# Up projection by seven products: the rounded and the low moving part of two products in one matmul of 512 columns

## The chip, the core and the metric

The kernel runs on one core of a Trainium2 chip. Its time is the device time of the whole kernel in microseconds, the median of the runs shown.

## What is computed

An encoder block on 512 tokens of width 2048: two groups of attention heads with one input and one output projection, then an MLP with squared ReLU. The change touches only the first matmul of the MLP:

```python
h = rms_norm(x, g_pre_mlp[l]) * (1.0 + sc_m) + sh_m       # (512, 2048)
y = jnp.square(jax.nn.relu(h @ w_mlp_in[l])) @ w_mlp_out[l]   # w_mlp_in (2048, 8192)
x = x + gt_m * rms_norm(y, g_post_mlp[l])
```

All of it is float32.

## The kernel before

**Float32 by three products.** Each float32 operand is held as a rounded part (type fp32r, names with `hi`) and what is left of it (`lo`). A product is the sum of three matmuls: rounded by rounded, rounded weight by low activations, low weight by rounded activations. ScalarE (ACT) makes the rounded part of a weight (`su_hi`, line 1303), VectorE (DVE) the low part (`su_low`, line 2053), in a ring of four slots `hi[s]`, `lo[s]` of 1024 columns.

**Seven products.** The up projection is done by blocks of 256 output features. After the first four, which are done plainly, there are 28 blocks (`SU_BLOCKS`). In each, the weight (2048 x 256) is seen as 2 x 2 quarters of 1024 x 128, and the transposed activations as 2 x 2 quarters of 1024 x 256, and the block is put together from seven products of a weight combination by an activation combination (Strassen's scheme in Winograd's form) in place of eight. A product is numbered `e`, 0 to 6. Its moving part is `B[e]` (line 2799), a rounded and a low half, each 8 slices (`KH`) of 256 columns (`HALF_T`). Products 3 and 6 take theirs from `h2_hi` and `h2_lo` directly (quarters 1,0 and 0,1; the second of these was overwritten with a combination).

**Where the sums go.** PSUM has banks of 512 float32 columns. A block uses half of three of them: X is bank 6 or 7 in turn, Y bank 4, Z bank 5. Products 0, 2, 4 and 6 add up in X, 1 and 5 in Y, 3 stands alone in Z. On the way ACT copies X after product 0, Y after product 1 and X after product 2 into `c_a` and `c_b` in SBUF (`snap` 0, 1, 2), and DVE adds Z after product 3, X after product 4 and Y after product 5 to them (`corner` 0, 1, 2). Product 6 leaves the last quarter in X, which ACT reads itself (`square_rest`).

**The order on each engine** is the order of the program, and semaphores tie them. In block i:
- PE: products 0 to 6. Product 2 waits for snap 0, product 4 for snap 2, product 6 for corner 1, product 1 for corner 2 of the block before, each product for the low part of its weight (`su_lo`).
- ACT: weight 3 rounded, `square_rest` of block i-1, snap 0, weight 4, snap 1, weight 5, snap 2, weight 6, y_out of block i-1 rounded (`pair_hi`), weights 0, 1 and 2 of block i+1, `square_tops` of block i. The rounding of a weight waits until the product four before has released the slot.
- DVE: low part 3, `sum_four`, low part 4, the four mixes of y of block i-1 (`mix_pair`), low part 5, a piece of the gate (`gate_part`), low part 6, low part of y_out of i-1 (`pair_lo`), corner 0, `sum_one` for block i+1, low part 0, corner 1, low part 1, `sum_two`, `sum_three`, corner 2, low part 2.
- SyncE issues the four loads of 512 KB of a block as the steps above free their buffers (line 649), GpSimd stores y_out.

`sum_one` to `sum_four` (line 2056) make the weight combinations, in SBUF. In the last group (`LAST`, the last four blocks) `mix_pair` does nothing, and y_out is done in two operations of 512 columns. The stage that follows is the down projection (`dn_products`, lines 2848 to 2850), whose matmuls all have 512 columns.

Of the kernel before, what the change touches and what calls it, by code (L numbers as in the profile page):

```python
# [27 lines left out]
T = 512  # L28
NT = T // P
D = 2048  # L30
KD = D // P
# [65 lines left out]
KH = KD // 2  # L97
# [59 lines left out]
def build(nc, a, out, x1_dram, y_dram):  # L157
    with ExitStack() as ctx:
# [14 lines left out]
        def small(name, shape):  # L173
# [50 lines left out]
        o_hi, o_lo = sb("o_hi", 52, [KD, T], F32R), sb("o_lo", 84, [KD, T], F32R)  # L224
        h2_hi, h2_lo = sb("h2_hi", 52, [KD, T], F32R), sb("h2_lo", 84, [KD, T], F32R)

# [48 lines left out]
                                 for n, ats in (("one", (152, 160)), ("two", (168, 196)), ("three", (142, 188))))  # L275
        four_f = quarter(sb("h2_lo_f", 84, [KD, T]), 0, 1)
        c_a, c_b = sb("c_a", 150, [2, HALF_T]), sb("c_b", 204, [2, HALF_T])
        rows_m = sb("rows_m", 204, [COLS])
# [197 lines left out]
        X = lambda i: bank[6 + i % 2][:, 0:HALF_T]  # L476
        Y, Z = bank[4][:, 0:HALF_T], bank[5][:, 0:HALF_T]

        def at_dn(g, np, u):
# [338 lines left out]
        def _(act):  # L818
# [486 lines left out]
            def snap(g, i, n):  # L1305

                dst, src = ((c_a[:, 0, :], X(i)), (c_b[:, 1, :], Y), (c_a[:, 1, :], X(i)))[n]
                act.wait_ge(w_used, at_su(g, i, n).count(1, 1))
                if n == 0 and not (isinstance(g, int) and su_count(g, i, 1) == 0):
                    act.wait_ge(y_done, pair_n(g, i, 2))  # L1310
                nc.scalar.activation(dst, src, ACT.Copy).then_inc(su_snap, 1)

            def square_tops(g, i):

                act.wait_ge(su_c, su_count(g, i, 3, 3))
                flat_a = c_a[:].rearrange("p a n -> p (a n)")
                nc.scalar.activation(flat_a, flat_a, ACT.Relu).then_inc(relu_done, 1)
                nc.scalar.activation(c_b[:, 1, :], c_b[:, 1, :], ACT.Relu, scale=-1.0).then_inc(relu_done, 1)
                act.wait_ge(relu_done, su_count(g, i, 2, 1 + 2 * SU_FIRST))
                act.wait_ge(y_ready, pair_n(g, i))  # L1320
                nc.scalar.activation(y_mix[:, 0:2, :].rearrange("p a n -> p (a n)"), flat_a, ACT.Square).then_inc(y_done, 1)

            def square_rest(g, i):

                act.wait_ge(w_used, at_su(g, i, 6).count(1, 1))
                nc.scalar.activation(c_b[:, 0, :], X(i), ACT.Relu, scale=-1.0).then_inc(su_x, 1)
                act.wait_ge(su_x, su_count(g, i, 1, 1))
                act.wait_ge(relu_done, su_count(g, i, 2, 2 + 2 * SU_FIRST))
                nc.scalar.activation(y_mix[:, 6:8, :].rearrange("p a n -> p (a n)"), c_b[:].rearrange("p a n -> p (a n)"), ACT.Square).then_inc(y_done, 1)
# [114 lines left out]
        def _(dve):  # L1444
# [633 lines left out]
            def corner(g, i, n):  # L2078

                dst, src, e = ((c_a[:, 0, :], Z, 3), (c_b[:, 1, :], X(i), 4), (c_a[:, 1, :], Y, 5))[n]  # L2080
                dve.wait_ge(w_used, at_su(g, i, e).count(1, 1))
                dve.wait_ge(su_snap, su_count(g, i, 3, n + 1))
                tt(dst, src, dst, ALU.add).then_inc(su_c, 1)  # L2083

# [8 lines left out]
            def su_block(g, i):  # L2093
# [3 lines left out]
                su_low(g, i, 3)  # L2097
                sum_four(g, i)
                su_low(g, i, 4)
                mix_pair(g, i - 1)  # L2100
# [51 lines left out]
            def finish(u):  # L2152

                if u == 0:
                    corner(LAST, PAIRS - 1, 2)
                if u == 5:
                    gate_part(LAST, PAIRS - 1)
# [177 lines left out]
        def _(pe):  # L2335
# [456 lines left out]
            def up_block(f, before=lambda j: None, rest=range(UNITS_D)):  # L2792
                for j in rest:
# [3 lines left out]
                    unit_columns(w, up_set(f), h2_hi, h2_lo, QROWS * j, j == 0, j == UNITS_D - 1)  # L2797

            B = (h2_at(0, 0), t_one, t_two, h2_at(1, 0), t_three, h2_at(1, 1), t_four)

            def su_block(g, i):

                first = isinstance(g, int) and su_count(g, i, 1) == 0
                into = (X(i), Y, X(i), Z, X(i), Y, X(i))
                for e in range(SLOTS):
                    w = at_su(g, i, e)
# [5 lines left out]
                    if e == 1:  # L2812
                        wait_su(pe, su_c, g, i, 3)
                    if e in (2, 4):
                        pe.wait_ge(su_snap, su_count(g, i, 3, e - 1))
                    if e == 6:
                        pe.wait_ge(su_c, su_count(g, i, 3, 2))
                    if first and e in (1, 6):
                        pe.wait_ge(t_ready, 3 if e == 1 else 4)
                    pe.wait_ge(su_lo, su_count(g, i, SLOTS, e + 1))  # L2820
                    s, opens = w.slot(), e in (0, 1, 3)
                    for k in range(KH):
                        cols = slice(k % 4 * P, (k % 4 + 1) * P)
                        wh, wl = hi[s][:, k // 4, cols], lo[s][:, k // 4, cols]
                        bh, bl = (x[:, k, :] for x in B[e])
                        mm(into[e], wh, bh, start=opens and k == 0, stop=False, skip_group_check=not opens)  # L2826
                        mm(into[e], wh, bl, start=False, stop=False, skip_group_check=not opens)  # L2827
                        ins = mm(into[e], wl, bh, start=False, stop=k == KH - 1, skip_group_check=not opens)  # L2828
# [43 lines left out]
            def free_banks(i):  # L2872
# [3 lines left out]
                if i == 2:  # L2876
                    pe.wait_ge(su_c, 3 * SU_BLOCKS)

# [260 lines left out]
```

## Time and profile before

| | |
|---|---|
| median of 3 runs | 2010.45 us (2009.76 to 2010.79) |
| profiled execution | 2010.1 us, span 2008.1 us |
| PE busy | 1980.6 us, 99% of the span |
| PE weight load busy | 1734.6 us, 86% |
| DVE busy | 1720.9 us, 86% |
| ACT busy | 1006.4 us, 50% |
| DMA | 433.31 MB, mean 216 GB/s |
| up projection by seven products | about 809 to 1376 us |
| down projection | about 1376 to 1992 us |

PE is TensorE's matmuls, DVE VectorE, ACT ScalarE, POOL GpSimd, SP SyncE. In the profile, a matmul's record is longer than the distance to the next one (0.28 us against 0.12), as matmuls are pipelined and their ends modelled: the cost of one is the distance between starts. The same holds in a smaller way for DVE and ACT, where records of chained operations overlap by 0.08 to 0.1 us. Idle time of an engine stands in square brackets behind the row of the operation that ended it, with what released it.

### The profile page before, as it was taken

How to read it: one execution, taken by the hardware profiler on the slowest of the kernel's cores; microseconds unless marked ns; L12 is line 12 of the kernel's file. 1: busy time of each engine (PE TensorE's matmuls, PEld its weight loads, DVE VectorE, ACT ScalarE, POOL GpSimd, SP SyncE). 2: the span in 40 equal slices, each digit the busy share in tenths (PEclk: the TensorE clock that was granted, in tenths of full speed). 3: DMA queues.
4: the chain of work that ended last, by engine and by line, in shares of the span. 5: the costliest groups of instructions: out<-in, count | busy, mean ns of one | idle time of the engine just before them, and what ended most of it. 6: DMA issues, size and time to landing. Idle time of an engine off the chain costs nothing.

```text
span 2008.1 us, 30631 instructions
## 1 busy us (share of the span) xinstructions
PE 1980.6 (99%) x11143; PEld 1734.6 (86%) x11143; DVE 1720.9 (86%) x2051; ACT 1006.4 (50%) x1425; POOL 159.8 (8%) x174
## 2 busy tenths in 40 slices
PE   7999999999999999999999999999999999999998
PEld 6887888878888878999999999998888888888886
DVE  7897988788877788999999999988998898898866
ACT  6464223698732474565656565655343334333322
POOL 0000000267400000000000000000300000000000
PEclk9999999999999999999999999999999999999999
DMA  9988778500487745667666767669746546556552
GB/s 378 351 299 304 249 218 254 180 1 22 150 268 255 239 157 189 216 213 232 211 233 210 234 208 233 210 207 349 242 173 251 205 171 251 191 185 251 179 177 84
DMA packets 260467, 433.31 MB, mean 216 GB/s; under 512 B 27680, under 2 KB 155296, under 8 KB 247456
## 3 DMA queue, kind: packets, MB, share of 16 engines
q1 hardware_dynamic: 242576, 361.42, 53.0%
q0 software_dynamic: 15936, 63.97, 8.7%
q10 hardware_dynamic: 1872, 6.82, 0.9%
q8 instruction: 52, 0.85, 0.2%
q14 instruction: 31, 0.25, 0.0%
HBM read 367.68 MB, written 64.49 MB: 215 GB/s over the span
## 4 chain that ended last, share of the span: by engine, by line
PE 90%; DVE 4%; ACT 3%; issue 1%; DMA 1%; SPq 0%; POOL 0%; ACTq 0%; POOLq 0%; DVEq 0%
PE bank L2826 9%; PE bank L2828 9%; PE bank L2827 9%; PE bank L2848 9%; PE bank L2850 9%; PE bank L2849 9%; PE bank L2349 6%; PE bank L2351 6%; PE bank L2350 6%; PE bank L2909 1%; PE bank L2908 1%; PE bank L2907 1%; PE bank L2364 1%; PE bank L2363 1%; PE bank L2362 1%
## 5 line engine op out<-in xcount | busy, mean ns | idle before, releaser
L1384 ACT ACTIVATE hi<-w 128x1024 fp32r<-128x1024 f32 x168 | 178.4, 1062 | 264.9 <-PE bank L2850 194.4
L2848 PE MATMUL bank<-hi,y_use 128*128 128x512 f32 x784 | 306.6, 391 | 0.0
L2849 PE MATMUL bank<-lo,y_use 128*128 128x512 f32 x784 | 305.1, 389 | 0.0
L2850 PE MATMUL bank<-hi,y_use 128*128 128x512 f32 x784 | 305.1, 389 | 0.0
L1303 ACT ACTIVATE hi<-a 128x1024 fp32r<-128x1024 f32 x196 | 206.6, 1054 | 154.5 <-DVE a L2056 142.0
L2053 DVE TENSOR_TENSOR lo<-a,hi 128x1024 fp32r<-128x1024 f32 x196 | 239.1, 1220 | 43.6 <-ACT hi L1303 43.2
L2826 PE MATMUL bank<-h_hi,hi 128*128 128x256 f32 x896 | 253.7, 283 | 1.0 <-DVE c_b L2083 1.0
L2828 PE MATMUL bank<-h_hi,lo 128*128 128x256 f32 x896 | 253.6, 283 | 0.0
L2827 PE MATMUL bank<-h_lo,hi 128*128 128x256 f32 x896 | 253.6, 283 | 0.0
L825 ACT ACTIVATE hi<-raw 128x1024 fp32r<-128x1024 f32 (+2 forms) x119 | 119.6, 1009 | 229.6 <-PE bank L2351 80.2
L2168 DVE TENSOR_TENSOR lo<-w,hi 128x1024 fp32r<-128x1024 f32 x168 | 205.2, 1228 | 31.3 <-ACT hi L1384 30.1
L1452 DVE TENSOR_TENSOR lo<-raw,hi 128x1024 fp32r<-128x1024 f32 (+2 forms) x118 | 135.6, 1151 | 62.4 <-ACT hi L825 61.2
L2849 PEld LDWEIGHTS bank<-lo,y_use 128*128 128x128 f32 x784 | 147.2, 188 | 31.4 <-issue 1.0
L2848 PEld LDWEIGHTS bank<-hi,y_use 128*128 128x128 f32 x784 | 147.2, 188 | 31.3 <-issue 1.0
L2850 PEld LDWEIGHTS bank<-hi,y_use 128*128 128x128 f32 x784 | 147.1, 188 | 30.7
L2826 PEld LDWEIGHTS bank<-h_hi,hi 128*128 128x128 f32 x896 | 172.0, 192 | 1.2 <-DVE c_b L2083 1.2
L2827 PEld LDWEIGHTS bank<-h_lo,hi 128*128 128x128 f32 x896 | 172.0, 192 | 0.0
L2828 PEld LDWEIGHTS bank<-h_hi,lo 128*128 128x128 f32 x896 | 172.0, 192 | 0.0
L2056 DVE TENSOR_TENSOR a<-a,a 128x1024 f32<-128x1024 f32 x112 | 134.5, 1221 | 2.0
L2248 DVE TENSOR_TENSOR acc<-bank,acc 128x1024 f32<-128x1024 f32 x84 | 102.3, 1217 | 0.0
L2349 PE MATMUL bank<-hi,h_hi 128*128 128x512 f32 x256 | 100.6, 393 | 0.7 <-DVE lo L1452 0.7
L2351 PE MATMUL bank<-hi,h_lo 128*128 128x512 f32 x256 | 99.7, 389 | 0.0
(406 smaller groups left out, 4690.3 us busy)
## 6 DMA issues: line engine op xcount, KB each, us to landing
w<-in_w_mlp_out SPq DMA_DIRECT2D x128, 512.0 KB, 4.9
a<-in_w_mlp_in SPq DMA_DIRECT2D x112, 512.0 KB, 4.5
y_use<-y_dram SPq DMA_DIRECT2D x53, 1024.0 KB, 9.1
y_dram<-y_out POOLq DMA_DIRECT2D x28, 1792.0 KB, 6.8
w_turned<-in_w_ada_t SPq DMA_DIRECT2D x32, 1024.0 KB, 6.9
raw<-in_w_mod SPq DMA_DIRECT2D x64, 512.0 KB, 4.8
raw<-in_w_ada SPq DMA_DIRECT2D x36, 512.0 KB, 4.7
raw<-in_w_out SPq DMA_DIRECT2D x32, 512.0 KB, 4.6
```

The source lines that it names most:

```text
L1303: nc.scalar.activation(hi[w.slot()][:], su_weight(i, e)[:].rearrange("p (q k) n -> p q (k n)", q=QROWS), ACT.Copy).then_inc(hi_ready, 1)
L1384: nc.scalar.activation(hi[w.slot()][:], weight(np, i, h)[:], ACT.Copy).then_inc(hi_ready, 1)
L2053: tt(lo[w.slot()][:], src, hi[w.slot()][:].bitcast(F32), ALU.subtract).then_inc(su_lo, 1)
L2168: tt(lo[w.slot()][:], weight(np, i, h)[:], hi[w.slot()][:].bitcast(F32), ALU.subtract).then_inc(dn_lo, 1)
L2349: mm(acc[t][:], xh, hi[s][:, q, :], start=first and q == 0, stop=False)
L2351: ins = mm(acc[t][:], xl, hi[s][:, q, :], start=False, stop=last and q == QROWS - 1)
L2826: mm(into[e], wh, bh, start=opens and k == 0, stop=False, skip_group_check=not opens)
L2827: mm(into[e], wh, bl, start=False, stop=False, skip_group_check=not opens)
L2828: ins = mm(into[e], wl, bh, start=False, stop=k == KH - 1, skip_group_check=not opens)
L2848: mm(bank[b + m][:], yh, hi[s][:, q, :], start=j == 0, stop=False)
L2849: mm(bank[b + m][:], yh, lo[s][:, q, :], start=False, stop=False)
L2850: ins = mm(bank[b + m][:], yl, hi[s][:, q, :], start=False, stop=j == PAIRS - 1)
```

## The change

Activations: `h2_hi` and `h2_lo` become the two halves of one tile `h2_pair`, at the same addresses. For products 3 and 6 a slice of the rounded and the same slice of the low activations are one moving operand of 2 x 256 columns, so that rounded weight by rounded and by low activations is one matmul of 512 columns into a whole bank: the left half gets the one, the right half the other. The third matmul, low weight by rounded activations, goes on into the left half, with 256 columns. The two halves are added by DVE when they are read (`tensor_reduce`).

Bank 5 now starts from a seed: snap 0 writes half of X into each half of it, bank to bank, in place of a copy to `c_a`. Corner 0 is the reduce of bank 5 into `c_a`. A new corner 3 is the reduce of the X bank after product 6 into `c_b`, done by DVE in the next block between `sum_four` and low part 4 (for the last block behind the second low part of the down stage). `square_rest` reads `c_b` and waits for corner 3; `su_c` counts four steps a block.

The diff:

```diff
@@ -222,7 +222,8 @@
         qr_even, qr_odd = sb("qr_even", 178, [HEADS // 2, T], F32R), sb("qr_odd", 168, [HEADS // 2, T], F32R)
         qr_round = sb("qr_round", 158, [T], F32R)
         o_hi, o_lo = sb("o_hi", 52, [KD, T], F32R), sb("o_lo", 84, [KD, T], F32R)
-        h2_hi, h2_lo = sb("h2_hi", 52, [KD, T], F32R), sb("h2_lo", 84, [KD, T], F32R)
+        h2_pair = sb("h2_pair", 52, [2, KD, T], F32R)
+        h2_hi, h2_lo = h2_pair[:, 0], h2_pair[:, 1]
 
         x_t = sb("x_t", 116, [KD, T])
         x_at = lambda k: x_t[:, KD - 1 - k, :]
@@ -274,6 +275,7 @@
         one_f, two_f, three_f = (tuple(sb(f"t_{n}_f{i}", at, [KH, HALF_T])[:] for i, at in enumerate(ats))
                                  for n, ats in (("one", (152, 160)), ("two", (168, 196)), ("three", (142, 188))))
         four_f = quarter(sb("h2_lo_f", 84, [KD, T]), 0, 1)
+        h2_both = lambda rows, cols: h2_pair[:, :, KH * rows:KH * (rows + 1), HALF_T * cols:HALF_T * (cols + 1)]
         c_a, c_b = sb("c_a", 150, [2, HALF_T]), sb("c_b", 204, [2, HALF_T])
         rows_m = sb("rows_m", 204, [COLS])
 
@@ -475,6 +477,9 @@
 
         X = lambda i: bank[6 + i % 2][:, 0:HALF_T]
         Y, Z = bank[4][:, 0:HALF_T], bank[5][:, 0:HALF_T]
+        halves_of = lambda b: b.rearrange("p (a n) -> p a n", a=2)
+        seeded = lambda x: bass.AP(x.tensor, x.offset, [list(x.ap[0]), [0, 2], [1, HALF_T]])
+        SU_C = 4
 
         def at_dn(g, np, u):
             if isinstance(g, int):
@@ -1304,15 +1309,18 @@
 
             def snap(g, i, n):
 
-                dst, src = ((c_a[:, 0, :], X(i)), (c_b[:, 1, :], Y), (c_a[:, 1, :], X(i)))[n]
                 act.wait_ge(w_used, at_su(g, i, n).count(1, 1))
-                if n == 0 and not (isinstance(g, int) and su_count(g, i, 1) == 0):
+                if n == 0:
+                    nc.scalar.activation(halves_of(bank[5]), seeded(X(i)), ACT.Copy, scale=0.5).then_inc(su_snap, 1)
+                    return
+                dst, src = ((c_b[:, 1, :], Y), (c_a[:, 1, :], X(i)))[n - 1]
+                if n == 1 and not (isinstance(g, int) and su_count(g, i, 1) == 0):
                     act.wait_ge(y_done, pair_n(g, i, 2))
                 nc.scalar.activation(dst, src, ACT.Copy).then_inc(su_snap, 1)
 
             def square_tops(g, i):
 
-                act.wait_ge(su_c, su_count(g, i, 3, 3))
+                act.wait_ge(su_c, su_count(g, i, SU_C, SU_C - 1))
                 flat_a = c_a[:].rearrange("p a n -> p (a n)")
                 nc.scalar.activation(flat_a, flat_a, ACT.Relu).then_inc(relu_done, 1)
                 nc.scalar.activation(c_b[:, 1, :], c_b[:, 1, :], ACT.Relu, scale=-1.0).then_inc(relu_done, 1)
@@ -1322,8 +1330,8 @@
 
             def square_rest(g, i):
 
-                act.wait_ge(w_used, at_su(g, i, 6).count(1, 1))
-                nc.scalar.activation(c_b[:, 0, :], X(i), ACT.Relu, scale=-1.0).then_inc(su_x, 1)
+                act.wait_ge(su_c, su_count(g, i, SU_C, SU_C))
+                nc.scalar.activation(c_b[:, 0, :], c_b[:, 0, :], ACT.Relu, scale=-1.0).then_inc(su_x, 1)
                 act.wait_ge(su_x, su_count(g, i, 1, 1))
                 act.wait_ge(relu_done, su_count(g, i, 2, 2 + 2 * SU_FIRST))
                 nc.scalar.activation(y_mix[:, 6:8, :].rearrange("p a n -> p (a n)"), c_b[:].rearrange("p a n -> p (a n)"), ACT.Square).then_inc(y_done, 1)
@@ -2077,10 +2085,13 @@
 
             def corner(g, i, n):
 
-                dst, src, e = ((c_a[:, 0, :], Z, 3), (c_b[:, 1, :], X(i), 4), (c_a[:, 1, :], Y, 5))[n]
+                dst, src, e = ((c_a[:, 0, :], bank[5], 3), (c_b[:, 1, :], X(i), 4), (c_a[:, 1, :], Y, 5), (c_b[:, 0, :], bank[6 + i % 2], 6))[n]
                 dve.wait_ge(w_used, at_su(g, i, e).count(1, 1))
-                dve.wait_ge(su_snap, su_count(g, i, 3, n + 1))
-                tt(dst, src, dst, ALU.add).then_inc(su_c, 1)
+                if n in (1, 2):
+                    dve.wait_ge(su_snap, su_count(g, i, 3, n + 1))
+                    tt(dst, src, dst, ALU.add).then_inc(su_c, 1)
+                else:
+                    nc.vector.tensor_reduce(dst, src.rearrange("p (a n) -> p n a", a=2), AX.X, ALU.add).then_inc(su_c, 1)
 
             def gate_part(g, i):
 
@@ -2096,6 +2107,8 @@
                 final = is_last(g, i) and i == PAIRS - 1
                 su_low(g, i, 3)
                 sum_four(g, i)
+                if not first:
+                    corner(g, i - 1, 3)
                 su_low(g, i, 4)
                 mix_pair(g, i - 1)
                 su_low(g, i, 5)
@@ -2153,6 +2166,8 @@
 
                 if u == 0:
                     corner(LAST, PAIRS - 1, 2)
+                if u == 1:
+                    corner(LAST, PAIRS - 1, 3)
                 if u == 5:
                     gate_part(LAST, PAIRS - 1)
                 if u == 6:
@@ -2796,12 +2811,14 @@
                     pe.wait_ge(raw_used, r.count(1, 1))
                     unit_columns(w, up_set(f), h2_hi, h2_lo, QROWS * j, j == 0, j == UNITS_D - 1)
 
+            B_BOTH = {3: h2_both(1, 0), 6: h2_both(0, 1)}
             B = (h2_at(0, 0), t_one, t_two, h2_at(1, 0), t_three, h2_at(1, 1), t_four)
 
             def su_block(g, i):
 
                 first = isinstance(g, int) and su_count(g, i, 1) == 0
                 into = (X(i), Y, X(i), Z, X(i), Y, X(i))
+                beside = {3: bank[5], 6: bank[6 + i % 2]}
                 for e in range(SLOTS):
                     w = at_su(g, i, e)
                     if e == 0:
@@ -2810,21 +2827,24 @@
                         else:
                             wait_su(pe, su_x, g, i, 1, -1)
                     if e == 1:
-                        wait_su(pe, su_c, g, i, 3)
+                        wait_su(pe, su_c, g, i, SU_C, -1)
                     if e in (2, 4):
                         pe.wait_ge(su_snap, su_count(g, i, 3, e - 1))
                     if e == 6:
-                        pe.wait_ge(su_c, su_count(g, i, 3, 2))
+                        pe.wait_ge(su_c, su_count(g, i, SU_C, 2))
                     if first and e in (1, 6):
                         pe.wait_ge(t_ready, 3 if e == 1 else 4)
                     pe.wait_ge(su_lo, su_count(g, i, SLOTS, e + 1))
-                    s, opens = w.slot(), e in (0, 1, 3)
+                    s, opens = w.slot(), e in (0, 1)
                     for k in range(KH):
                         cols = slice(k % 4 * P, (k % 4 + 1) * P)
                         wh, wl = hi[s][:, k // 4, cols], lo[s][:, k // 4, cols]
                         bh, bl = (x[:, k, :] for x in B[e])
-                        mm(into[e], wh, bh, start=opens and k == 0, stop=False, skip_group_check=not opens)
-                        mm(into[e], wh, bl, start=False, stop=False, skip_group_check=not opens)
+                        if e in beside:
+                            mm(halves_of(beside[e]), wh, B_BOTH[e][:, :, k, :], start=False, stop=False, skip_group_check=True)
+                        else:
+                            mm(into[e], wh, bh, start=opens and k == 0, stop=False, skip_group_check=not opens)
+                            mm(into[e], wh, bl, start=False, stop=False, skip_group_check=not opens)
                         ins = mm(into[e], wl, bh, start=False, stop=k == KH - 1, skip_group_check=not opens)
                     ins.then_inc(w_used, 1)
 
@@ -2874,7 +2894,7 @@
                 if i == 0:
                     pe.wait_ge(relu_done, 4 * PLAIN_BLOCKS)
                 if i == 2:
-                    pe.wait_ge(su_c, 3 * SU_BLOCKS)
+                    pe.wait_ge(su_c, SU_C * SU_BLOCKS - 1)
 
             def free_gate_banks(i):
```

## Rows read from the trace of the kernel before

**Rows 1.** Windows: stretch; us and busy us (operations) by engine; clock; DMA
```profile
809.00:1377.00 568.00, 567.00 (x4715) 566.38 (x4714) 512.00 (x552) 338.99 (x454) 26.77 (x29) 1.00 0.69 223
12.00:18.00 6.00, 5.03 (x31) 5.03 (x32) 4.13 (x8) 4.18 (x8) 0.00 (x0) 0.72 1.01 425
...
694.00:712.00 18.00, 15.38 (x72) 12.39 (x71) 13.43 (x21) 15.35 (x30) 0.57 (x3) 1.00 0.47 189
```

**Rows 2.** Timeline of PE, products: start, us, line, operation (34 starts between)
```profile
999.83 0.28 PE L2826 MATMUL bank<-t_two_hi,hi 128*128 128x256 f32 x1
...
1003.91 0.28 PE L2827 MATMUL bank<-h_lo,hi 128*128 128x256 f32 x1
```

**Rows 3.** Timeline of DVE, one block and the ends of it
```profile
1015.73 1.23 DVE L2053 TENSOR_TENSOR lo<-a,hi 128x1024 fp32r<-128x1024 f32 x1 [1.34 <-ACT hi L1303]
...
1018.16 1.23 DVE L2053 TENSOR_TENSOR lo<-a,hi 128x1024 fp32r<-128x1024 f32 x1
1019.30 0.42 DVE L1998 TENSOR_TENSOR y_mix<-y_mix 128x256 f32<-128x256 f32 x1
...
1020.77 1.22 DVE L2053 TENSOR_TENSOR lo<-a,hi 128x1024 fp32r<-128x1024 f32 x1
...
1023.10 1.22 DVE L2053 TENSOR_TENSOR lo<-a,hi 128x1024 fp32r<-128x1024 f32 x1
1024.58 2.03 DVE L2012 TENSOR_TENSOR y_out<-y_mix,y_out 128x1792 fp32r<-128x1792 f32 x1 [0.27 <-ACT y_out L1285]
...
1032.99 0.42 DVE L2083 TENSOR_TENSOR c_a<-bank,c_a 128x256 f32<-128x256 f32 x1
...
1035.88 1.23 DVE L2053 TENSOR_TENSOR lo<-a,hi 128x1024 fp32r<-128x1024 f32 x1 [1.34 <-ACT hi L1303]
```

**Rows 4.** Timeline of ACT, the same block
```profile
1015.60 0.36 ACT L1326 ACTIVATE c_b<-bank 128x256 f32<-128x256 f32 x1
1016.07 0.63 ACT L1329 ACTIVATE y_mix<-c_b 128x512 f32<-128x512 f32 x1
1016.79 0.39 ACT L1311 ACTIVATE c_a<-bank 128x256 f32<-128x256 f32 x1
1017.07 1.05 ACT L1303 ACTIVATE hi<-a 128x1024 fp32r<-128x1024 f32 x1
...
1021.63 0.38 ACT L1311 ACTIVATE c_a<-bank 128x256 f32<-128x256 f32 x1 [1.55 <-PE bank L2828]
...
1033.44 0.64 ACT L1317 ACTIVATE c_a<-c_a 128x512 f32<-128x512 f32 x1 [0.41 <-DVE c_a L2083]
...
1034.81 1.04 ACT L1303 ACTIVATE hi<-a 128x1024 fp32r<-128x1024 f32 x1
```

**Rows 5.** Timeline of DVE, starts of the second and third block
```profile
834.66 1.23 DVE L2053 TENSOR_TENSOR lo<-a,hi 128x1024 fp32r<-128x1024 f32 x1 [1.34 <-ACT hi L1303]
...
854.44 1.23 DVE L2053 TENSOR_TENSOR lo<-a,hi 128x1024 fp32r<-128x1024 f32 x1 [1.34 <-ACT hi L1303]
```

**Rows 6.** Timeline of PE, down projection, 512 columns (14 starts between)
```profile
1599.65 0.39 PE L2848 MATMUL bank<-hi,y_use 128*128 128x512 f32 x1
...
1602.82 0.39 PE L2850 MATMUL bank<-hi,y_use 128*128 128x512 f32 x1
```

**Rows 7.** Groups of instructions of the whole span: busy us, mean ns, idle before
```profile
L1756 DVE TENSOR_REDUCE top<-bank 128x1 f32<-128x512 f32 x64 | 43.3, 680 | 2.1 <-PE bank L2583 1.5
...
L1213 ACT ACTIVATE bank<-part 128x512 f32<-128x512 f32 x4 | 2.4, 602 | 4.0 <-DVE part L1907 3.4 <-issue 0.4
```

**Rows 8.** Timeline of DVE, starts of the third last and the last block
```profile
1318.12 1.23 DVE L2053 TENSOR_TENSOR lo<-a,hi 128x1024 fp32r<-128x1024 f32 x1 [1.34 <-ACT hi L1303]
...
1357.48 1.23 DVE L2053 TENSOR_TENSOR lo<-a,hi 128x1024 fp32r<-128x1024 f32 x1 [1.34 <-ACT hi L1303]
```

**Rows 9.** Groups of instructions, 900 to 1400 us: half of a short y_out
```profile
L2009 DVE TENSOR_TENSOR y_out<-y_mix,y_out 128x512 fp32r<-128x512 f32 x4 | 2.7, 685 | 0.0
```

**Rows 10.** Timeline of PE, first matmul of the down projection
```profile
1375.67 0.40 PE L2848 MATMUL bank<-hi,y_use 128*128 128x512 f32 x1
```

## The prediction

> **What bounds the kernel now.** I read the windows first, to see which engine fills the stage that the change touches (the up projection by seven products, 809 to 1377 us): the matrix engine is busy for 567 of 568 us, the vector engine for 512, the scalar engine for 339, at full granted clock [rows 1]. So PE sets the pace and DVE stands close behind. The timeline of PE says what a product costs: 34 starts of 256-column matmuls in 4.08 us, 0.120 us each [rows 2]. A product has 24 of them (8 slices of the contraction, three matmuls each), 2.88 us, and a block of seven products 20.16 us; there are 28 blocks. Then I asked how far behind DVE really is, by reading its timeline over one block. Its first step of a block, the low part of the fourth weight, I call T; T is at 1015.73, and the next at 1035.88, which is 20.15 later [rows 3]. In between it idles 0.27 us before the low half of y_out and 1.34 us before T. The first is a wait for PE's pace by way of ACT (ACT copies the X bank after the third product, at 1021.63, and only then rounds weight 6 and y_out) [rows 4]. The second is no slack. It is the way from DVE's third corner (1032.99) through ACT's three squares and relus to the rounding of the next fourth weight (1034.81) and back to T (1035.88), 2.89 us whatever PE does [rows 3, 4]. Without PE, DVE and ACT together need T to low part of weight 4 2.43, on to the end of low part 6 6.08 (1018.16 to 1023.10, and 1.14 as a chained 1024-column operation takes), y_out to third corner 8.41, and 2.89: 19.81 us. One block of the trace shows this loop running free: the second, where T goes from 834.66 to 854.44, 19.78 us [rows 5]. So the reserve under PE's 20.16 is 0.35 us a block, not the tenth that the busy shares suggest.
>
> **The part on PE.** Products 3 and 6 (counted from 0) lose two matmuls of 256 columns per slice and gain one of 512; the columns stay the same. 512-column matmuls start 14 times in 3.17 us, 0.2264 us each [rows 6]; two of 256 take 0.240. Saved: 0.0136 a slice, 16 slices a block, 0.22 us a block; a block becomes 19.94 us and 28 blocks save 6.1 us. The new moving operand is in two pieces, 32 KB apart, which no row shows: between 0.226 (a contiguous one) and 0.240 (two matmuls), and I take 0.227. What hides an error here is said below: PE gets 3.4 us of idle time in each block.
>
> The Trainium skill ("TensorE: Matmul & The Clock Gate", section "Wait — 56ns, not 53.3ns?") gives a matmul at full clock its columns at 2.4 GHz plus about 2.5 ns. By that figure 448 matmuls fewer would save 1.1 us in all, and the first rival below would come to 2009.4. The rows show 120 ns for 256 columns where the columns alone are 106.7, so 13.3 ns each, and the measurement decides.
>
> **The parts on DVE.** Corner 0 was a sum of a bank half and c_a, 256 columns, 0.42 us, of which the next operation sees 0.33. It becomes a tensor_reduce over the 512 columns of bank 5. The nearest row is the reduce of a 128x512 bank, 0.680 us [rows 7]; with the same overlap of 0.08 the next operation starts 0.60 later: +0.26 (0.27 by the two starts). A second such reduce, corner 3, is new: +0.60. Bounds of both: 0.42 if only results count, 0.94 if 512 reads and 256 writes are paid one after the other; I take the measured 0.68, whose reads are the same. The address changes cost nothing.
>
> **The part on ACT, and the wait that it brings.** Snap 0 was a copy of 256 columns and becomes 512 columns, bank to bank. The nearest row that writes a bank is a square of 128x512, 0.602 us [rows 7], against 0.39; bounds 0.39 and 0.70. The costly edit is one line in square_rest. Before, it waited for product 6 of the last block, done long ago. Now it waits for corner 3, which DVE does only in the *next* block: after the low part of weight 3 (T) and sum_four, so at T+2.43 to T+3.11. Behind square_rest in ACT's queue stand snap 0 and the rounding of weight 4, and DVE's very next operation after corner 3 is the low part of weight 4, which needs that rounding. So DVE waits for a chain that it has just released itself:
> - first relu of square_rest 3.14, second operation 3.62, snap 0 4.12 (0.42 to 0.47 and 0.54 between starts, as at 1015.60 and 1016.07 [rows 4]; the old snap waited for the end of the square, the new one doesn't, so 0.50 stands for its 0.72),
> - rounding of weight 4 from 4.62 to 5.67 (1.05), low part of weight 4 at T+5.70.
> Before it stood at T+2.43. Of the 3.27 that it comes later, 0.60 is the reduce and 2.67 is idle DVE time with nothing to fill it, as the mixes of y stand behind it.
>
> **The sum.** The loop without PE becomes 19.81 + 0.26 + 0.60 + 2.67 = 23.34 us a block, against PE's 19.94. DVE and ACT become the bound. Check that nothing on PE holds it up: PE's third product waits for snap 0, T+4.8; products 2 to 5 end at T+16.2 (4.8 + 2.88 + 2.77 + 2.88 + 2.88); product 6 waits for corner 1, T+17.07, and ends at T+19.84. The next fourth weight may be rounded then, and is due at T+22.3. ACT's copy after product 2 is free at T+7.9 and y_out rounded at T+10.8, before DVE asks at T+11.8: the 0.27 wait is gone. The transfers keep their distances, as the steps that free their buffers move with T. PE idles some 2.5 us before product 2 and 0.9 before product 6.
> Over the stage: the first T doesn't move. The second is later by 0.26 (834.92). Blocks 1 to 24 take 24 x 23.34 = 560.2, so the T of block 25 is at 1395.1, where it was 1318.12 [rows 8]. The last blocks skip the four mixes (1019.30 to 1020.77, 1.47 us [rows 3]) and split a y_out of quarter size into two operations of 0.685 (0.60 chained, 1.20 against 1.95 [rows 9]), and wait 0.1 for a rounding that comes last then: 23.34 - 1.47 - 0.75 + 0.1 = 21.22 us each, two of them, T of block 27 at 1437.5 (was 1357.48). PE ends that block 19.0 after T (no wait for corner 1 there: 4.8 and five products), at 1456.5; its first down product started at 1375.67 [rows 10]. That is +80.8 us. In the down stage corner 3 puts 0.6 us on DVE once, in front of low parts that are done 1 to 2 us before PE needs them: 0, at most 0.6. The profiled execution took 2010.1 us (its span 2008.1 and 2.0 around it), 0.35 under the median of 2010.45. So 2010.1 + 80.8 = 2090.9, on the median 2091.3.
>
> **The rivals.**
> - *PE stays the bound and the gain is had.* This needs ACT to round weight 4 without having waited for corner 3, and DVE's additions to fit. Then 28 x 0.22 = 6.1 us off: 2004.3. It decides from the point where the DVE loop is under 19.94. For it speaks only DVE's busy share of 90%; against it the free loop of 19.78, which 0.13 us would fill while the reduces alone bring 0.86. 4%.
> - *Only the added work counts, the wait is covered.* The loop is 19.81 + 0.86 = 20.67, so +0.53 on 25 blocks: 2023.5. It needs 2.67 us of other work between corner 3 and weight 4, which the order of the code doesn't have. 5%.
> - *The clock falls.* PE would be idle in 3.4 of 23.3 us, 15%. Early in the kernel, where the inputs are transposed, six microseconds show a mean clock of 0.72 with PE 84% busy; but 18 us ahead of the MLP, PE 85% busy too, show 1.00 [rows 1]. At 1.2 GHz the columns of a block (43008) take 35.8 us instead of 17.9. The idle 3.4 us pays for 19% of a block at the low level; beyond that it decides. With half of each block low, 9.0 - 3.4 = 5.6 us x 27 = 150 more: 2242. 6%. The Trainium skill speaks for this one (the same page, "A second HAM failure mode: psum-queue depth-cycling": short idle times between groups of matmuls make the clock swing between its levels); the 18 us at 1.00 speak against it.
> - *The change doesn't do what it says*, PE takes 0.240 for the combined matmul or more: the forecast stays, as PE has 3.4 us to lose. Time within 0.2% of before would need the loop to grow by exactly the reserve: 1%.
>
> **How the numbers follow.** The forecast has 84%. Its bounds: both reduces at 0.42 take 0.52 off 26 blocks, 13.5 us, and a snap at 0.39 another 5: 2072. Reduces at 0.94 and a snap at 0.70 add 14 and 2.6: 2108. These two ends are the range, as the other cases (4, 5, 6 and 1%) lie outside and hold 16%. What a measurement of this kernel can tell from no change is 0.2%, 4 us. Faster by more: 4%; within: 2%; slower: 94%.
>
> **What would show it.** Right: 512-column matmuls at 0.227 in products 3 and 6; the distance of T to T 23.3; about 2.7 us idle on DVE before the low part of weight 4, released by ACT; PE idle before product 2 for snap 0, 2.5 us a block; ACT idle before square_rest, released by the vector engine's reduce; the stage some 81 us longer and the others unchanged. Wrong: T to T near 20 with PE never idle; reduces far from 0.68; a granted clock under 0.95 in the stage.

## The result and the profile after

The changed kernel takes 2108.41 us (median of 4 runs, 2107.06 to 2110.78) against 2010.55 us: the ratio is 1.0489 (95% interval 1.0471 to 1.0507), 98 us slower. The forecast was 2091.3 us with a range up to 2108.0: the direction and most of the size are right, and the time lies just past the upper end. The profiled execution took 2107.06 us, its span is 2105.1.

The page of the changed kernel, busy time by engine and the first line of the chain that ended last:

```profile
PE 2015.2 (96%) x10695; PEld 1741.6 (83%) x10695; DVE 1746.6 (83%) x2079; ACT 1011.0 (48%) x1425; POOL 160.7 (8%) x174
...
PE 66%; DVE 15%; ACT 9%; issue 8%; DMA 1%; ACTq 0%; DVEq 0%; SPq 0%; POOL 0%; POOLq 0%
```

TensorE (PE) is busy for 96% of a longer span. Of the chain, 66% are PE's. In the middle of the stage it is plain that PE waits, and something stands there that the kernel before never showed in this stage [rows 1]: a granted clock under 1 (0.94, where the forecast had named a clock under 0.95 as a sign that it is wrong). Windows, with the columns of rows 1:

```profile
850.00:1400.00 550.00, 495.82 (x3519) 473.12 (x3518) 448.42 (x486) 281.65 (x369) 22.61 (x24) 0.94 0.57 187
```

One block on VectorE (DVE). T, the low part of weight 3, is the first row, the next T the last:

```profile
1000.97 1.23 DVE L2061 TENSOR_TENSOR lo<-a,hi 128x1024 fp32r<-128x1024 f32 x1 [1.34 <-ACT hi L1308]
...
1003.37 0.68 DVE L2094 TENSOR_REDUCE c_b<-bank 128x256 f32<-128x512 f32 x1
1006.74 1.23 DVE L2061 TENSOR_TENSOR lo<-a,hi 128x1024 fp32r<-128x1024 f32 x1 [2.69 <-ACT hi L1308]
...
1013.33 2.02 DVE L2020 TENSOR_TENSOR y_out<-y_mix,y_out 128x1792 fp32r<-128x1792 f32 x1 [0.36 <-ACT y_out L1290]
1015.28 0.68 DVE L2094 TENSOR_REDUCE c_a<-bank 128x256 f32<-128x512 f32 x1
...
1022.01 0.42 DVE L2092 TENSOR_TENSOR c_a<-bank,c_a 128x256 f32<-128x256 f32 x1
...
1024.90 1.23 DVE L2061 TENSOR_TENSOR lo<-a,hi 128x1024 fp32r<-128x1024 f32 x1 [1.34 <-ACT hi L1308]
```

The forecast's chain is there, term by term. The reduce for corner 3 takes 0.68 us; then DVE is idle for 2.69 us (forecast 2.67) until weight 4 is rounded, and the low part of weight 4 stands at T+5.77 (forecast 5.70). From y_out to the third corner it is 8.68 us (forecast 8.67), from there to T 2.89. But T to T is 23.93, not 23.34, and the y_out at 1013.33 is still preceded by an idle time that should have gone (0.36 us, as 0.27 in [rows 3]). The same block on ScalarE (ACT):

```profile
999.89 1.04 ACT L1308 ACTIVATE hi<-a 128x1024 fp32r<-128x1024 f32 x1
1004.09 0.42 ACT L1334 ACTIVATE c_b<-c_b 128x256 f32<-128x256 f32 x1 [3.15 <-DVE c_b L2094]
1004.62 0.63 ACT L1337 ACTIVATE y_mix<-c_b 128x512 f32<-128x512 f32 x1
1005.16 0.58 ACT L1314 ACTIVATE bank<-bank 128x512 f32<-128x512 f32 x1
1005.67 1.03 ACT L1308 ACTIVATE hi<-a 128x1024 fp32r<-128x1024 f32 x1
...
1010.38 0.39 ACT L1319 ACTIVATE c_a<-bank 128x256 f32<-128x256 f32 x1 [2.46 <-PE bank L2848]
...
1011.61 1.69 ACT L1290 ACTIVATE y_out<-y_mix 128x1792 fp32r<-128x1792 f32 x1
```

ACT waits 3.15 us for the reduce, and then the squares, snap 0 (0.58 us, bank to bank) and weight 4 follow as counted. What is late is the copy of X after product 2, at 1010.38: T+9.41 where the forecast had T+7.9. PE says why:

```profile
1003.30 0.28 PE L2848 MATMUL bank<-t_one_hi,lo 128*128 128x256 f32 x1
1005.86 0.58 PE L2846 MATMUL bank<-t_two_hi,hi 128*128 128x256 f32 x1 [2.28 <-ACT bank L1314]
1006.24 0.41 PE L2847 MATMUL bank<-t_two_lo,hi 128*128 128x256 f32 x1
1006.45 0.41 PE L2848 MATMUL bank<-t_two_hi,lo 128*128 128x256 f32 x1
...
1008.59 0.41 PE L2846 MATMUL bank<-t_two_hi,hi 128*128 128x256 f32 x1
1008.80 0.35 PE L2847 MATMUL bank<-t_two_lo,hi 128*128 128x256 f32 x1
1008.99 0.28 PE L2848 MATMUL bank<-t_two_hi,lo 128*128 128x256 f32 x1
1009.10 0.28 PE L2846 MATMUL bank<-t_two_hi,hi 128*128 128x256 f32 x1
...
1010.18 0.40 PE L2844 MATMUL bank<-h_pair,hi 128*128 128x512 f32 x1
```

After 2.28 us of waiting for snap 0, PE starts matmuls of 256 columns every 0.213 us: the low one of the two levels, 1.2 GHz. Only after some 2.9 us does the distance return to 0.12. Windows over two such stretches, in this block and in one where the clock held:

```profile
1005.80:1008.80 3.00, 2.94 (x14) 2.94 (x14) 2.06 (x4) 2.12 (x3) 0.00 (x0) 0.50 0.42 125
1053.70:1056.70 3.00, 2.99 (x25) 3.00 (x26) 2.11 (x4) 2.07 (x3) 0.00 (x0) 1.00 0.40 118
```

So product 2 took 4.1 to 4.5 us instead of 3.0 in 20 of the 25 blocks in which PE idles about 2.0 to 2.3 us before it, and 3.0 us in the five others; in those five T to T is 23.40 us. In the last two, with 0.94 us of idle time, the clock held as well. The groups of these operations, over the whole span:

```profile
L2846 PE MATMUL bank<-t_two_hi,hi 128*128 128x256 f32 x224 | 80.0, 357 | 57.4 <-ACT bank L1314 57.4
...
L2094 DVE TENSOR_REDUCE c_b<-bank 128x256 f32<-128x512 f32 x28 | 19.1, 682 | 0.0
L2094 DVE TENSOR_REDUCE c_a<-bank 128x256 f32<-128x512 f32 x28 | 19.1, 682 | 0.0
...
L1314 ACT ACTIVATE bank<-bank 128x512 f32<-128x512 f32 x28 | 16.2, 580 | 0.0
```

The first of the three matmuls of a slice of product 2 takes 357 ns on the mean, against 283 before; both reduces at 682 ns, as the row of the attention part had it [rows 7].

### The profile page after: what moved, and what is told of

The parts are those of the page before. It is cut to its first block, busy times and chain, and to the rows that moved or that the text cites. A ratio compares the mean times of both kernels' runs of the same rounds, so it can differ in the third digit from the quotient of the medians.

```text
span 2105.1 us, 29745 instructions
## 1 busy us (share of the span) xinstructions
PE 2015.2 (96%) x10695; PEld 1741.6 (83%) x10695; DVE 1746.6 (83%) x2079; ACT 1011.0 (48%) x1425; POOL 160.7 (8%) x174
## 4 chain that ended last, share of the span: by engine, by line
PE 66%; DVE 15%; ACT 9%; issue 8%; DMA 1%; ACTq 0%; DVEq 0%; SPq 0%; POOL 0%; POOLq 0%
PE bank L2868 8%; PE bank L2870 8%; PE bank L2869 8%; DVE lo L2061 5%; PE bank L2364 5%; PE bank L2366 5%; PE bank L2365 5%; DVE a L2064 3%; ACT hi L1308 2%; PE bank L2846 2%; PE bank L2848 2%; PE bank L2847 2%; ACT y_out L1290 1%; PE bank L2929 1%; PE bank L2928 1%
## 5 line engine op out<-in xcount | busy, mean ns | idle before, releaser
L2848 PE MATMUL bank<-h_pair,lo 128*128 128x256 f32 x896 | 252.7, 282 | 0.0
L2848 PEld LDWEIGHTS bank<-h_pair,lo 128*128 128x128 f32 x896 | 170.9, 191 | 0.0
L2844 PE MATMUL bank<-h_pair,hi 128*128 128x512 f32 x448 | 162.2, 402 | 4.4 <-DVE c_b L2092 4.4
L2846 PE MATMUL bank<-t_two_hi,hi 128*128 128x256 f32 x224 | 80.0, 357 | 57.4 <-ACT bank L1314 57.4
L2847 PE MATMUL bank<-h_pair,hi 128*128 128x256 f32 x448 | 126.8, 283 | 0.0
L2846 PE MATMUL bank<-h_pair,hi 128*128 128x256 f32 x448 | 126.7, 283 | 0.0
L2846 PEld LDWEIGHTS bank<-t_two_hi,hi 128*128 128x128 f32 x224 | 55.8, 249 | 62.8 <-issue 49.1
L2844 PEld LDWEIGHTS bank<-h_pair,hi 128*128 128x128 f32 x448 | 84.9, 189 | 23.8 <-DVE lo L2061 3.9
```

Source lines behind the costliest of these rows:

```text
L2844: mm(halves_of(beside[e]), wh, B_BOTH[e][:, :, k, :], start=False, stop=False, skip_group_check=True)
```

## Experiments

The first four were measured beside each other, against the kernel before at 2010.77 us.

**wait_only.** The wait without the matmuls, in the kernel before:

```diff
+                if n == 3:
+                    dve.wait_ge(w_used, at_su(g, i, 6).count(1, 1))
+                    nc.vector.tensor_copy(c_b[:, 0, :], X(i)).then_inc(su_c, 1)
+                    return
...
-                act.wait_ge(w_used, at_su(g, i, 6).count(1, 1))
-                nc.scalar.activation(c_b[:, 0, :], X(i), ACT.Relu, scale=-1.0).then_inc(su_x, 1)
+                act.wait_ge(su_c, su_count(g, i, 4, 4))
+                nc.scalar.activation(c_b[:, 0, :], c_b[:, 0, :], ACT.Relu, scale=-1.0).then_inc(su_x, 1)
```

> The kernel before, with one thing of the change alone: VectorE copies the last quarter from the X bank to c_b in the next block (256 columns, at the place of the new corner 3), and square_rest on ScalarE waits for that copy. All matmuls, snap 0 and corner 0 stay as before. Theory (the wait is the loss): the low part of weight 4 comes at T+5.4 in place of T+2.43, 2.6 us of it idle on VectorE, so T to T is 22.8 us where the clock holds, some 0.5 more where it falls; 25 blocks by 2.7 to 3.2 us: 2077 to 2092 us. Rival (the loss is in the combined matmuls, their two-piece operand or the reduces): only 0.33 us of work is added, within the reserve: 2010 to 2012 us.

Measured 2085.44 us, ratio 1.0369 (1.0351 to 1.0386). DVE:

```profile
1044.08 1.23 DVE L2053 TENSOR_TENSOR lo<-a,hi 128x1024 fp32r<-128x1024 f32 x1 [1.34 <-ACT hi L1303]
...
1046.48 0.42 DVE L2082 COPY c_b<-bank 128x256 f32<-128x256 f32 x1
1049.54 1.23 DVE L2053 TENSOR_TENSOR lo<-a,hi 128x1024 fp32r<-128x1024 f32 x1 [2.64 <-ACT hi L1303]
```

One copy of 0.42 us costs 75 us, because 2.64 us of idle time stand behind it in each block. This alone is three quarters of the whole loss. T to T is 22.8 us, and 23.3 to 23.5 in the 7 blocks in which the clock fell. PE idles less before product 2 here: 1.8 to 2.0 us in 18 blocks, and the 7 are among these; in the 9 others it is 0.5 to 1.6 us, and the clock held.

**reordered.** All of the change; only ACT's and DVE's order differs:

```diff
                 if first:
                     square_pair(SU_FIRST - 1)
-                else:
-                    square_rest(g, i - 1)
                 snap(g, i, 0)
                 su_hi(g, i, 4)
+                if not first:
+                    square_rest(g, i - 1)
...
                 su_low(g, i, 4)
+                if not first:
+                    gate_part(g, i - 1)
                 mix_pair(g, i - 1)
```

> The changed kernel with all its matmuls, reduces and the bank seed; only the order differs. On ScalarE snap 0 and the rounding of weight 4 stand ahead of square_rest, on VectorE the piece of the gate stands ahead of the four mixes. So weight 4 no longer waits for corner 3, and the mixes have 1.2 us more until the squares are done. Theory (the wait is the loss): the loop of VectorE and ScalarE is 19.81 + 0.26 + 0.60 = 20.67 us, T to T 20.7, TensorE idle 0.7 us a block at full clock: 2022 to 2026 us. Rival (the work of the change is the loss): stays near 2100 us.

Measured 2022.51 us, ratio 1.0060 (1.0043 to 1.0077): 86 of the 98 us are back, with each matmul and reduce in place.

```profile
1000.42 1.23 DVE L2061 TENSOR_TENSOR lo<-a,hi 128x1024 fp32r<-128x1024 f32 x1 [1.35 <-ACT hi L1308]
...
1002.83 0.68 DVE L2094 TENSOR_REDUCE c_b<-bank 128x256 f32<-128x512 f32 x1
1003.42 1.22 DVE L2061 TENSOR_TENSOR lo<-a,hi 128x1024 fp32r<-128x1024 f32 x1
...
1021.04 1.23 DVE L2061 TENSOR_TENSOR lo<-a,hi 128x1024 fp32r<-128x1024 f32 x1 [1.34 <-ACT hi L1308]
```

Low part 4 follows the reduce at once, and T to T is 20.62 (worked out beforehand: 20.67). The clock is 1.00 in the whole stage. What is left of the loss is the 0.86 us of reduces in a loop that had 0.35 to spare.

**filler.** The changed kernel, PE kept at work while it waits:

```diff
+                    if e == 2 and not first:
+                        for _ in range(16):
+                            mm(bank[0][:, 0:HALF_T], h2_hi[:, 0, 0:P], h2_hi[:, 0, 0:HALF_T], start=True, stop=True)
```

> The changed kernel with 16 idle-time matmuls of 256 columns (1.92 us at full clock, into a bank that nobody reads in this stage) on TensorE ahead of the wait for snap 0, in each block but the first. They fill 1.9 of the 2.3 us in which it waits there. Theory (what exceeds the 23.34 us of the forecast is TensorE's clock after that idle time): product 2 takes 2.9 us in every block in place of 4.3 us in 20 of them, T to T is 23.4 in all, and the kernel takes 2094 to 2098 us, though TensorE has more to do. Rival (the clock doesn't hang on the idle time, or the 0.5 us come from elsewhere): 2108 us or more.

Measured 2095.63 us, ratio 1.0422 (1.0404 to 1.0439), 12.8 us less than the changed kernel, with 432 matmuls more. PE, and a window over product 2:

```profile
1001.61 2.08 PE L2833 MATMUL bank<-h_pair 128*128 128x256 f32 x16
1004.10 0.38 PE L2849 MATMUL bank<-t_two_hi,hi 128*128 128x256 f32 x1 [0.41 <-ACT bank L1314]
```

```profile
1004.00:1007.00 3.00, 2.90 (x24) 2.91 (x25) 2.02 (x4) 2.16 (x3) 0.00 (x0) 1.00 0.40 121
```

0.41 us of idle time is left, the clock stays at its high level in every block, and T to T is 23.32 to 23.41 in the 24 blocks with mixes, 23.40 in most. The forecast's 23.34 was the loop at full clock; the fall of the clock was the missing part.

**three_only.** The change for product 3 alone (product 6, `square_rest` and the count of `su_c` as before):

```diff
-            B_BOTH = {3: h2_both(1, 0), 6: h2_both(0, 1)}
+            B_BOTH = {3: h2_both(1, 0)}
```

> The change for product 3 alone: combined matmul, bank seed and reduce for bank 5; product 6 and square_rest as before, no corner 3. Theory: TensorE needs 20.16 - 0.11 = 20.05 us a block, the loop of VectorE and ScalarE 19.81 + 0.26 = 20.07; without the wait nothing stalls, so 28 blocks by 0.1 less: 2006 to 2010 us, slightly faster than before. Rival (the combined matmul or the seed costs by itself): above 2013 us.

Measured 2010.59 us, ratio 0.9996 (0.9987 to 1.0006): no difference, 0.6 us above what the theory gave (a gain that this interval doesn't show) and under the rival's bound. PE has no wait over 0.1 us in the steady blocks; DVE has none either but for ACT's squares:

```profile
1018.19 1.23 DVE L2061 TENSOR_TENSOR lo<-a,hi 128x1024 fp32r<-128x1024 f32 x1 [1.34 <-ACT hi L1308]
...
1020.66 1.23 DVE L2061 TENSOR_TENSOR lo<-a,hi 128x1024 fp32r<-128x1024 f32 x1
...
1038.31 1.23 DVE L2061 TENSOR_TENSOR lo<-a,hi 128x1024 fp32r<-128x1024 f32 x1 [1.34 <-ACT hi L1308]
```

T to T is 20.12, DVE's loop with one reduce (20.07 was worked out), 0.04 under the 20.16 of before. So this half of the change costs nothing and gives nothing that can be measured. Which engine now sets the 20.12 the trace doesn't tell: by the distances measured (0.354 us a slice, see below) PE needs 20.11 itself.

**reordered_pool, pool_mix_before, three_only_pool.** Could the combined matmuls gain if DVE had less to do? First by giving the four mixes of y to GpSimd, in the reordered kernel (there with the low half of y_out behind low part 0), in the kernel before and in three_only:

```diff
+                        if not is_last(g, j) and not (isinstance(g, int) and pair_n(g, j) < SU_FIRST):
+                            mix_on_pool(g, j)
                         save_pair(g, f, pr)
```

> The reordered kernel (all of the change, no wait on weight 4), with the four mixes of y moved from VectorE to GpSimd from the fifth block on, and the low half of y_out put behind the low part of weight 0. Theory: with VectorE's loop at 20.62 - 1.47 = 19.15 us, TensorE's 19.94 is the bound for the first time and the gain of the combined matmuls shows: 28 blocks by 0.22 us, 2003 to 2007 us, T to T 19.9. Rival (the combined matmul gains nothing, or GpSimd's mixes of some 0.65 us each, half of its 128x512 rows of 1.29, come too late for y_out or slow VectorE down): 2010 us or more.

> The kernel before, with the four mixes of y on GpSimd from the fifth block on and nothing else. TensorE bounds the stage there without a wait, so every theory in which TensorE is the bound expects no change: 2009 to 2012 us. If it were faster, the gain of the reordered kernel on GpSimd would come from the mixes and not from the matmuls. If the mixes on GpSimd are late: slower.

> The change for product 3 alone, with the mixes on GpSimd. VectorE's loop falls from 20.12 to about 18.7 us, TensorE needs 20.05 a block: 28 blocks by 0.11 us less than before, 2006.5 to 2009 us, half of what both products give. If the combined matmul gains nothing: 2010 to 2012 us.

Measured 2082.54 us (1.0363, 1.0349 to 1.0378), 2013.59 us (1.0015, 1.0006 to 1.0024) and 2020.99 us (1.0049, 1.0035 to 1.0063). What was expected missed in all three; the second lies 1.6 us above its range. GpSimd's timeline in reordered_pool:

```profile
1023.63 1.64 POOL L3084 TENSOR_TENSOR y_mix<-y_mix 128x256 f32<-128x256 f32 x1 [9.37 <-ACT y_mix L1337]
1025.23 1.72 POOL L3085 TENSOR_TENSOR y_mix<-y_mix 128x256 f32<-128x256 f32 x1
1026.91 1.72 POOL L3087 TENSOR_TENSOR y_mix<-y_mix 128x256 f32<-128x256 f32 x1
1028.71 1.81 POOL L3089 TENSOR_TENSOR y_mix<-y_mix 128x256 f32<-128x256 f32 x1
```

A mix of 128x256 takes 1.7 us there while DVE works, not the 0.65 that I had by halving the 128x512 rows of the attention part; four of them 6.9 us against 1.5 on DVE. In reordered_pool y_out comes late, and ACT, in order, holds the weights behind it. In the two others y_out isn't late; what grew there is DVE's own work. Both engines in three_only_pool:

```profile
1002.01 0.76 POOL L3077 TENSOR_TENSOR y_mix<-y_mix 128x256 f32<-128x256 f32 x1 [8.93 <-ACT y_mix L1337]
1002.20 1.65 DVE L2064 TENSOR_TENSOR a<-a,a 128x1024 f32<-128x1024 f32 x1
1007.13 1.76 DVE L2102 SCALAR_TENSOR_TENSOR gm_acc<-gate_row,silu_c,gm_acc 128x1024 f32<-128x1024 f32 x1
```

The sum takes 1.65 us beside the mixes instead of 1.22, the gate 1.76 instead of 1.28, each of the two low parts between them (3.44 us together) 1.76 instead of 1.22: 2.0 us more in a block, for 1.47 us of mixes taken away. So DVE's loop grows by 0.5, from 20.12 to some 20.6 (T to T is 20.56), and in pool_mix_before from 19.81 to some 20.3 (20.30, over PE's 20.16). GpSimd's adds and DVE's slow each other. None of the three says anything on the matmuls.

**gate_fill, gate_fill_before.** Better to fill DVE's own idle 1.34 us before T with the piece of the gate (1.2 us), and to leave the mixes:

```diff
                 corner(g, i, 2)
                 su_low(g, i + 1, 2)
+                if not first:
+                    gate_part(g, i - 1)
```

> All of the change, snap 0 and weight 4 ahead of square_rest on ScalarE as in the reordered kernel, no GpSimd mixes; the piece of the gate moves on VectorE to the end of the block, behind the low part of weight 2, into the 1.34 us in which it waits there for ScalarE's squares and weight 3. Theory: VectorE's loop is 20.62 - 1.20 + 0.15 (the mixes wait a little for the squares) = 19.6 us, under TensorE's 19.94, which becomes the bound: T to T 19.94, no idle on TensorE, 28 blocks by 0.22 us less: 2003 to 2007 us. Rival (the combined matmul in a stage without stalls gains nothing): T to T 20.16 or more, 2010 us or more.

> The kernel before with the piece of the gate moved in the same way and nothing else: a control. TensorE bounds the stage without a wait, so VectorE's shorter loop gives nothing: 2009 to 2012 us. If it is faster by some 6 us, the gain of the other kernel comes from the gate's place and not from the matmuls.

Measured 2009.74 us (ratio 0.9995, 0.9986 to 1.0004) and 2010.37 us (1.0000, 0.9991 to 1.0009). The control is as expected. The first misses its 2003 to 2007: all of the change now costs nothing, but it gains nothing that can be measured either. DVE in gate_fill:

```profile
994.82 1.28 DVE L2102 SCALAR_TENSOR_TENSOR gm_acc<-gate_row,silu_c,gm_acc 128x1024 f32<-128x1024 f32 x1
996.25 1.23 DVE L2061 TENSOR_TENSOR lo<-a,hi 128x1024 fp32r<-128x1024 f32 x1
...
1004.80 2.03 DVE L2020 TENSOR_TENSOR y_out<-y_mix,y_out 128x1792 fp32r<-128x1792 f32 x1 [0.37 <-ACT y_out L1290]
...
1016.36 1.23 DVE L2061 TENSOR_TENSOR lo<-a,hi 128x1024 fp32r<-128x1024 f32 x1
```

T to T is 20.11. The idle time before T is down from 1.34 to 0.15 us, and the loop has closed elsewhere: DVE waits 0.37 us for the rounded y_out, behind a chain that again begins at corner 3 (square_rest, snap 1, weight 5, snap 2, weight 6, y_out on ACT).

**late_y, late_y_contiguous.** The y_out wait out of the way, and the same with the moving operand in one piece:

```diff
                 sum_one(g, i + 1)
+                if not first:
+                    pair_lo(g, i - 1)
                 su_low(g, i + 1, 0)
...
-                            mm(halves_of(beside[e]), wh, B_BOTH[e][:, :, k, :],
+                            mm(beside[e], wh, h2_hi[:, k, :],
```

> The gate_fill kernel, in which VectorE still waited 0.37 us for the rounded y_out (T to T about 20.1), with the low half of y_out moved behind sum_one. Theory: VectorE's loop is 19.75 us, and TensorE becomes the bound. But the traces so far show a combined matmul at 0.2365 us and the 256 columns behind it at 0.117, 0.354 a slice against 0.360, in place of the 0.347 of the forecast; so TensorE needs 20.06 us a block and the whole gain is 28 x 0.10 = 2.8 us: 2007 to 2009 us. Rival (the forecast's 0.2264 holds once nothing else binds): 19.94 a block, 2004 to 2006 us. Second rival: VectorE's order still binds, 2010 us.

> The late_y kernel, with 512 contiguous columns of the rounded activations as moving operand of the combined matmuls in place of the two pieces 32 KB apart. This computes something else (the low part of the activations is left out in products 3 and 6 and wrong columns stand in its place), but has the same count, sizes and weights of matmuls. Theory (the two pieces cost the 0.010 us over the 0.2264 of the down projection): 512 to 256 columns 0.2264 to 0.228, a block 19.95 us, 2004 to 2006 us. Rival (it is the change between 512 and 256 columns): as late_y, 0.2365.

Measured 2019.18 us (1.0040, 1.0027 to 1.0054) and 2019.00 us (1.0042, 1.0028 to 1.0055). As a faster version it failed: the second rival of late_y holds, and by more than it said. With y_out moved ahead of corner 1, product 6 waits for that corner in 9 blocks (up to 1.3 us), corner 0 for product 3, and sum_one for a transfer (up to 1.5 us in a block); the stage is 9 us longer than in gate_fill. But the second kernel, which leaves the low part of the activations out of products 3 and 6, answers what it was made for. PE in it, one slice:

```profile
1006.17 0.40 PE L2849 MATMUL bank<-h_pair,hi 128*128 128x512 f32 x1
1006.40 0.28 PE L2853 MATMUL bank<-h_pair,lo 128*128 128x256 f32 x1
1006.52 0.40 PE L2849 MATMUL bank<-h_pair,hi 128*128 128x512 f32 x1
```

Without the first slice of a product, which can stand behind a wait, the start of a 512-column matmul and the next start are 0.236 us apart, and the start of a 256-column one and the next 0.117, on the mean of over 300 distances each; with the operand in two pieces, in late_y, 0.236 and 0.117 too. The pieces cost nothing, which is what the rival said. The extra 0.01 us over the 0.2264 of the down projection [rows 6] comes where 512 and 256 columns take turns; why, no run says.

## Why the forecast was right, and where it was wrong

**What bounds the kernel.** Right. A loop of DVE and ACT at 19.8 us stood 0.35 us behind PE's 20.16, and wait_only and reordered show both sides of it: 0.86 us of work more costs 12 us, an added wait 75.

**The parts on DVE and ACT, the wait.** Right to 0.08 us in each term: the reduces 0.68, the idle time 2.69 for 2.67, low part 4 at T+5.77 for T+5.70. At full clock T to T is 23.40 for 23.34.

**The part on PE.** The time of the combined matmul was mis-sized, with its sign right. The 0.2264 was taken from a row in which 512 columns follow 512. Between matmuls of 256 it is 0.2365, with 0.117 behind it, 0.354 a slice against 0.360 before: 0.10 us a block, 2.8 us in all where 6.1 were worked out. PE was not the bound, so this did not touch the sum. It does mean that the change could never have been worth more than 0.14%, and that the first rival, at 2004.3, was out of reach.

**The sum.** The step that failed is the check that PE holds nothing up. It counted product 2 at 2.88 us, the time at full clock, behind an idle time of 2.5 us and so had ACT's third copy at T+7.9, 1.0 us ahead of need. The third rival, the clock, was set up as a case by itself, with half of each block at the low level, a break-even point at 19% of the block, and 6%. The trace shows it small and nearly always: 13 to 16 matmuls of product 2, a tenth or less of a block's columns, in 20 of 25 blocks. And the break-even point was wrong: the 3.4 us of slack per block (2.8 in the trace at full clock: 2.25 before product 2 and 0.59 before product 6) were spread over two places, while on the way from product 2 to y_out there was 1.0 by the forecast and 0.9 in the trace. The 1.4 us lost in product 2 used that up and came out as 0.5 us a block. The clock belonged into the upper end of the range, not into a rival. (A slip in the second rival: 20.67 is 0.51 above 20.16, not 0.53, which gives 2023.2.)

Of the 16.2 us between the 2090.9 forecast for the profiled execution and its 2107.06 (the terms add up to it within 0.1): 11.2 are this (24 blocks at 23.81 on the mean in place of 23.40, 9.8 us, and 1.4 in the block after them; filler, where the clock holds, is 12.8 us faster, with a shorter wait in the down stage too); 1.4 the 0.06 us in 24 blocks (23.40 for 23.34); 0.8 a later T of the second block, of which 0.6 are there already when the stage begins; 0.5 the last block; 2.2 the down stage, where PE waits 1.9 us once, some 11 us after its first matmul, and the trace doesn't say for what. (PE had no wait there before; of the loads of y_use issued at the start of the stage, three took 13.1 to 17.2 us to land, where three had taken 10.0 to 13.8.)

**The two rules cited.** The Trainium skill's figure in "TensorE: Matmul & The Clock Gate", section "Wait — 56ns, not 53.3ns?" (0.0025 us per matmul beyond its columns) is not what these float32 matmuls show at either size: 13.3 ns at 256 columns and 13.1 at 512 (0.2264 us). The other rule of the Trainium skill (the same page, "A second HAM failure mode: psum-queue depth-cycling") was right against the 18 us at clock 1.00 that I set against it: it is short waits between groups of matmuls, repeated, that brought the clock down here. I weighed them by PE's mean busy share (85% in both), and the row that I compared with said nothing on how its idle time was cut into pieces.

## What to carry to other kernels

Before a step is handed from one in-order engine to another, write down what stands behind the waiting instruction and whether the releasing engine needs any of it next: here a 0.4 us copy became 75 us, since the engine that released the wait was the one that needed what was queued behind it. Fixing the order gave back 86 of 98 us with no work removed. Measure the reserve of the second engine by a block where it runs free, not by its busy share (90% busy, reserve 2%). And where a forecast has TensorE waiting for 2 us again and again, count the matmuls behind each wait at the low clock, and look at who waits for exactly those.

## What the runs showed of the hardware

- Waits of about 2.0 to 2.3 us on PE, once in a block, were followed by a stretch at the low level (2.9 us of matmuls in the block shown) in 20 of 25 cases in the changed kernel; waits of 1.8 to 2.0 us in 7 of 18 in wait_only; waits of 2.4 to 2.6 us in 5 of 8 and of 3.2 to 3.6 us in 6 of 6 in reordered_pool. No wait under 1.7 us was followed by one, in this stage of any kernel here.
- A tensor_reduce of 512 bank columns to 256 results takes 0.682 us, as one to a single result does (0.680): the number of results made no difference, and neither did the strided reads, 1 KB apart.
- ScalarE copies 512 columns from bank to bank, reading 256 twice, in 0.58 us.
- A 512-column float32 matmul takes 0.2264 us among its like and 0.236 between 256-column ones, its moving operand in one piece or in two.
- GpSimd adds two tiles of 128x256 in 1.6 to 1.8 us while VectorE works (the first of four in three_only_pool in 0.76), VectorE in 0.42. VectorE's own operations of 1.22 to 1.28 us take 1.65 to 1.76 beside those adds.
